# Attention values with the values as stationary operand, two branches in the two column halves, and sums transposed back

## The reference, cut to what matters

```python
s = jnp.einsum('bhgqd,bhqnkd->bhgqnk', qc, kg).astype(f32) * scale
p = masked_softmax(...)
o_sel = jnp.einsum('bhgqm,bhqmd->bhgqd', p, vg)
...
o_win = jnp.einsum('bhgcqk,bckhd->bcqhgd', p_w, vwin)
...
o_attn = gates[..., 0:1] * o_cmp + gates[..., 1:2] * o_sel + gates[..., 2:3] * o_win
```

## Time and profile before

| | |
|---|---|
| median of 3 runs | 605.27 us |
| lowest, highest | 604.96, 605.53 us |
| the profiled execution | 605.03 us |
| its span, first to last instruction | 603.3 us |
| granted TensorE clock over the span | 0.999 |
| PE busy | 591.7 us, 98% |
| DVE busy | 390.0 us, 65% |
| ACT busy | 299.9 us, 50% |
| POOL busy | 94.8 us, 16% |
| attention stage | 145.4 to 260.1 us |

### The profile page before, as it was taken

One profiled execution on the slowest core, in us unless ns is written; L12 is line 12 of the kernel. 1 busy time (PEld: TensorE's weight loads), 2 busy tenths in 40 slices (PEclk: granted clock), 3 DMA queues, 4 the chain that ended last, 5 costly groups with the idle time before them and its releaser, 6 DMA issues.

```text
span 603.3 us, 8925 instructions
## 1 busy us (share of the span) xinstructions
PE 591.7 (98%) x3009; PEld 494.1 (82%) x3009; DVE 390.0 (65%) x653; ACT 299.9 (50%) x533; POOL 94.8 (16%) x150
## 2 busy tenths in 40 slices
PE   8999999999999999999999999999999999999997
PEld 7777777888898889988888888888888888888885
DVE  3799862686688577656445434454368777788766
ACT  6865543638465667544323332233246555565561
POOL 1550000122222232222222122220000000000000
PEclk9999999999999999999999999999999999999999
DMA  8934247387878677777888888884326566555563
GB/s 308 325 94 140 93 160 252 108 290 186 240 147 226 141 148 211 116 181 170 246 222 205 262 199 230 216 201 122 105 92 200 197 185 197 174 153 179 193 207 139
DMA packets 33596, 112.51 MB, mean 186 GB/s; under 512 B 4560, under 2 KB 4848, under 8 KB 30752
## 3 DMA queue, kind: packets, MB, share of 16 engines
q1 hardware_dynamic: 28176, 72.56, 36.5%
q0 software_dynamic: 5248, 39.58, 28.7%
q10 hardware_dynamic: 144, 0.00, 0.0%
HBM read 110.03 MB, written 39.85 MB: 248 GB/s over the span
## 4 chain that ended last, share of the span: by engine, by line
PE 84%; DVE 6%; DMA 3%; issue 2%; POOL 2%; ACT 2%; SPq 1%; ACTq 0%; DVEq 0%
PE ps L356 23%; PE ps L358 23%; PE ps L357 23%; PE ps L1953 4%; PE ps L1941 2%; DMA xT<-in_xt 1%; PE ps L1903 1%; PE ps L1812 1%; PE ps L1904 1%; DMA pe_sb<-in_cmp_pe 1%; POOL rope_k L519 1%; PE ps L1669 1%; DVE ht_lo L1123 1%; PE ps L1775 1%; PE ps L1884 1%
## 5 line engine op out<-in xcount | busy, mean ns | idle before, releaser
L356 PE MATMUL ps<-ht_hi,w_hi_sb 128*128 128x512 f32 (+1 forms) x280 | 107.7, 385 | 0.0
L358 PE MATMUL ps<-ht_hi,w_lo_sb 128*128 128x512 f32 (+1 forms) x280 | 107.3, 383 | 0.0
L357 PE MATMUL ps<-ht_lo,w_hi_sb 128*128 128x512 f32 (+1 forms) x280 | 107.3, 383 | 0.0
L1030 ACT ACTIVATE w_hi_sb<-raw 128x1024 fp32r<-128x1024 f32 (+1 forms) x64 | 61.1, 954 | 61.1 <-PE ps L358 61.1
L1556 DVE TENSOR_TENSOR w_lo_sb<-raw,w_hi_sb 128x1024 fp32r<-128x1024 f32 (+1 forms) x64 | 68.5, 1089 | 32.5 <-ACT w_hi_sb L1030 32.3
L358 PE MATMUL ps<-w_hi_sb,a_lo 128*128 128x512 f32 x224 | 87.2, 389 | 0.0
L357 PE MATMUL ps<-w_lo_sb,a_hi 128*128 128x512 f32 x224 | 87.2, 389 | 0.0
L356 PE MATMUL ps<-w_hi_sb,a_hi 128*128 128x512 f32 x224 | 87.1, 389 | 0.0
L356 PE MATMUL ps<-w_hi_sb,ht_hi 128*128 128x512 f32 x192 | 81.6, 425 | 1.5 <-DVE w_lo_sb L1090 0.9
L1529 DVE TENSOR_TENSOR aq<-aq (+1 forms) x32 | 22.1, 692 | 86.3 <-ACT aq L1016 52.0
L358 PE MATMUL ps<-w_hi_sb,ht_lo 128*128 128x512 f32 x192 | 75.3, 392 | 0.0
(11 more groups left out here) (211 smaller groups left out, 922.3 us busy)
## 6 DMA issues: line engine op xcount, KB each, us to landing
raw<-in_w_ff SPq DMA_DIRECT2D x48, 512.0 KB, 4.3
forms<-in_w_ff POOLq DMA_DIRECT2D x32, 512.0 KB, 4.8
raw<-forms SPq DMA_DIRECT2D x32, 512.0 KB, 3.7
forms<-in_w_ff POOLq DMA_DIRECT2D x48, 256.0 KB, 4.8
raw<-in_w SPq DMA_DIRECT2D x23, 512.0 KB, 4.7
forms<-forms POOLq DMA_DIRECT2D x32, 256.0 KB, 5.0
xs<-in_x SPq DMA_DIRECT2D x8, 512.0 KB, 9.6
raw<-in_cmp_w SPq DMA_DIRECT2D x8, 512.0 KB, 4.5
```

What stands on the lines that cost most here:

```text
L356: pe.matmul(out, l_hi, r_hi, start=start, stop=False)
L357: pe.matmul(out, l_hi, r_lo, start=False, stop=False)
L358: return pe.matmul(out, l_lo, r_hi, start=False, stop=stop)
L1030: act.activation(w_hi_sb[:, FS[slot], 0:n], raw[:, slot, 0:n], ACT.Copy).then_inc(w_hi, 1)
```

## The change

The values of all steps but the last four are computed in another arrangement.

- Four steps (two heads, both branches) form a group `q` of 16; `QLAST` is 15, so 15 groups are new and the last four steps run in `last_values` as before, now into bank 6. The transposed probabilities of a group are kept in `pt_even` or `pt_odd`, eight slots in all.
- `values(q, ks)` (L1995 of the changed kernel): for each key tile `k` two products, one for each branch. The 64 columns of `v_sb` are the stationary operand, and the transposed probabilities of both heads move, 256 columns. The branch `b` writes to partitions `64 b` to `64 b + 63` of bank 7, in the column half `q % 2`. A group is cut into visits by `PARTS`: 1, 2, 3 and 3 of them for `t` = 0, 1, 2 and 3 (the last visit of `t = 3` takes two key tiles), one visit in a step.
- `ot(q)` on ACT (L980): copies the 128x256 sums to `ot_sb`, in the pass behind that of the last visit, after `exp(s + 2)` of that pass.
- `back(q)` on PE (L2014): two transposes of 128x128 from `ot_sb` to bank 6, so that the queries are in the partitions again. It waits for `ot_evac` and stands first in the second step behind the last visit, ahead of `scores(v + 2)`.
- `combine` reads bank 6 alone, waits for `back_done`, and moves to the passes 11, 19, 28, 36, 45, 53, 61 and 65 (before: 9, 17, 25, and so on). `norm_sum` and `norm_root` of the attention rows move with it: 19, 35, 51 to 20, 37, 54.

```diff
+GROUP = 4
+NQ = NV // GROUP
+QLAST = NQ - 1
+PARTS = {q: [[[0]], [[0], [1]], [[0], [1], [2]], [[0], [1], [2, 3]]][STEPS[GROUP * q][0]] for q in range(QLAST)}
+VALUES = {GROUP * q + GROUP - 1 + LAG + i: (q, ks) for q in PARTS for i, ks in enumerate(PARTS[q])}
+WHOLE = {q: GROUP * q + GROUP - 2 + LAG + len(PARTS[q]) for q in PARTS}
+BACK = {v + 2: q for q, v in WHOLE.items()}
+COMBINE = {v: q // 2 for v, q in BACK.items() if q % 2}
+COMBINE[NV + LAG - 1] = NQ // 2 - 1
...
             def pt(v):
                 n = P * (STEPS[v][0] + 1)
                 act.wait_ge(pt_done, v + 1)
-                if v >= 3:
-                    act.wait_ge(pv_done, v - 2)
-                act.activation(pt_sb[:, v % 3, 0:n], ps[:, 4 + v % 2, 0:n], ACT.Copy).then_inc(pt_evac[1], 1)
+                wait_pt_slot(act, v)
+                act.activation(pt_slot(v, n), ps[:, 4 + v % 2, 0:n], ACT.Copy).then_inc(pt_evac[1], 1)
+
+            def ot(q):
+
+                act.wait_ge(ot_done, q + 1)
+                if q >= 2:
+                    act.wait_ge(back_done, q - 1)
+                act.activation(ot_sb[:, q % 2, :, :].rearrange("p h s -> p (h s)"),
+                               ps[:, 7, q % 2 * 256:q % 2 * 256 + 256], ACT.Copy).then_inc(ot_evac, 1)
...
                 if w < NV:
                     exp(w)
+                if s - 1 in whole:
+                    ot(whole[s - 1])
                 if 0 <= s < NV and s % 2 == 1:
                     pt(s)
...
-                if s == 35:
+                if s == 37:
                     norm_root("attn", 0, 2)
-                if s == 51:
+                if s == 54:
                     norm_root("attn", 2)
...
-            def values(v):
+            def values(q, ks):
...
+                if ks[0] == 0:
+                    for b in range(NB):
+                        pe.wait_ge(pt_evac[b], 2 * q + 2)
...
+                for k in ks:
+                    for b in range(NB):
+                        pt = pt_odd[b] if q % 2 else pt_even[:, b, :, :]
+                        mm = pe.matmul(ps[HD * b:HD * b + HD, 7, cols], v_sb[:, k, b, g * HD:g * HD + HD],
+                                       pt[:, :, k * P:k * P + P], start=k == 0, stop=k == t)
+                if ks[-1] == t:
+                    mm.then_inc(ot_done, 1)
...
+            def back(q):
+
+                pe.wait_ge(ot_evac, q + 1)
...
+                if q % 2 == 0:
+                    wait_combined(q // 2)
+                for h in range(2):
+                    c = (q % 2 * 2 + h) * P
+                    mm = pe.transpose(ps[:, 6, c:c + P], ot_sb[:, q % 2, h, :], ident[:, :])
+                mm.then_inc(back_done, 1)
...
             for v in range(NV + LAG):
+                if v in BACK:
+                    back(BACK[v])
                 if v + LEAD < NV:
                     scores(v + LEAD)
...
-                if v >= LAG:
-                    values(v - LAG)
+                if v in VALUES:
+                    values(*VALUES[v])
+                if v - LAG >= GROUP * QLAST:
+                    last_values(v - LAG)
```

More of the change, by code:

```diff
@@ L132 @@
 SBANKS = 3
+GROUP = 4
[7 more added lines that the diff above has]
+COMBINE[NV + LAG - 1] = NQ // 2 - 1
+assert len(VALUES) == sum(map(len, PARTS.values())) and len(BACK) == QLAST and len(COMBINE) == NQ // 2
 PAIRED = NH * NB
@@ L263, in hybrid_block @@
         rope_sb = at("rope_sb", [P, NT, 2, HD], F32, o_gsgu + NG * HD * 4)
+        o_ones = area(0)
         ones = sb("ones", [P, P])
@@ L283, in hybrid_block @@
         pe_sb = sb("pe_sb", [P, 2, 16])
+        assert o_ones + 2 * SEQ * 4 <= top[0]
+        ot_sb = sb("ot_sb", [P, 2, 2, P])
         gate_t = at("gate_t", [GW, SEQ], F32, o_o + 3 * D * 4 + 2048)
@@ L402, in wait_out, with pt_slot, wait_pt_slot @@
                 eng.wait_ge(out_done, OUT_NO[s] + 1)
+        def pt_slot(v, n):
+            q, h, b = v // GROUP, v // 2 % 2, v % 2
+            return pt_odd[b][:, h, 0:n] if q % 2 else pt_even[:, b, h, 0:n]
+        def wait_pt_slot(eng, v):
+            if v >= 2 * GROUP:
+                eng.wait_ge(ot_done, v // GROUP - 1)
         def bc(ap, shape):
@@ L953, in job_act @@
                     ht_hi_evac(*k)
+            whole = {v: q for q, v in WHOLE.items()}
             exp(0)
@@ L1486, in _ @@
                     f_lo((s - 43) // 5, 2 * NS + (s - 43) // 5 + 1)
-                if s == 36:
+                if s == 38:
                     norm_inv("attn", 0, 2)
-                if s == 52:
+                if s == 55:
                     norm_inv("attn", 2)
@@ L1492, in _ @@
                     coefs(s // 16, s // 8 % 2)
-                if s >= 8 and s % 8 == 1:
-                    combine((s - LAG) // 16, (s - LAG) // 8 % 2)
+                if s in COMBINE:
+                    combine(COMBINE[s] // 2, COMBINE[s] % 2)
                 if s in (41, 45, 52, 56):
@@ L1942, in probs_t @@
                 mm.then_inc(pt_done, 1)
-            def values(v):
-                t, h, b = STEPS[v]
[L1946 to L1951, removed]
+            def values(q, ks):
+                t, h, _ = STEPS[GROUP * q]
+                g, cols = h // GQA, slice(q % 2 * 256, q % 2 * 256 + 256)
+                if ks[0] == 0:
+                    for b in range(NB):
+                        pe.wait_ge(pt_evac[b], 2 * q + 2)
+                    if q == 0:
+                        wait_free(pe, LAST_FILL[3])
+                    if q >= 2:
+                        pe.wait_ge(ot_evac, q - 1)
+                for k in ks:
[5 more added lines that the diff above has]
+                    mm.then_inc(ot_done, 1)
@@ new lines, in wait_combined @@
+            def wait_combined(group):
+                if group:
+                    pe.wait_ge(o_step, 5 * (group - 1) + 4)
+            def back(q):
+                pe.wait_ge(ot_evac, q + 1)
+                if q == 0:
+                    wait_free(pe, LAST_FILL[2])
+                if q % 2 == 0:
[4 more added lines that the diff above has]
+                mm.then_inc(back_done, 1)
@@ L1952, in values, with last_values @@
+            def last_values(v):
+                t, h, b = STEPS[v]
+                pe.wait_ge(pt_evac[b], v // 2 + 1)
+                wait_combined(NQ // 2 - 1)
+                c = h % 4 * P + b * HD
                 for k in range(t + 1):
-                    mm = pe.matmul(ps[:, 6 + h // 4, c:c + HD], pt_sb[:, v % 3, k * P:k * P + P],
-                                   v_sb[:, k, b, g * HD:g * HD + HD], start=k == 0, stop=k == t)
-                mm.then_inc(pv_done, 1)
+                    mm = pe.matmul(ps[:, 6, c:c + HD], pt_slot(v, SEQ)[:, k * P:k * P + P],
+                                   v_sb[:, k, b, h // GQA * HD:h // GQA * HD + HD], start=k == 0, stop=k == t)
+                mm.then_inc(pv_last, 1)
```

18 lines of the change are left out of this document (10 added, 8 removed).

## The result

The changed kernel takes **623.73 us** (median of 4 runs, 622.88 to 626.9) against 605.12 us (4 runs of the kernel before beside it, 604.93 to 605.53). The ratio is 1.0311, with a 95% interval of 1.0292 to 1.033: slower by 18.6 us, where the prediction said 11.3 us. The time lies in the predicted range, close to its upper end.

The account below looks back on a forecast made before the run. PE, busy for 98% of the span, was taken as the bound: 605.03 - 32.3 (old values) + 30.5 (new work) + 17.1 (waiting) - 4 (present stalls) gave 616.3 us, +11.3; range for 8 in 10: 606.5 to 624.

Parts of the forecast that it names:

- PE's own work: Attention stage: 32.3 us of old value records leave, 30.5 us of products, edges and transposes come; shrinks by 1.8 us.
- The edges: Entering and leaving the column halves on PE: 0.35 us for each of 33 visits, 11.6 us, priced from the L1812 block.
- The first rival: Faster, 602.7 us: edges cost nothing and the wait eats all 6 us of present stalls; chance 0.07.
- the second: Rival of no change, 604.4 us: edges at half price and only 11 us of the waiting left; chance 0.05.
- The wait: PE's `back` waits for ACT's copy behind scores, row maximum and exponential within one step, at 14 places: 17.1 us.
- the third rival: Worse, 626 us: the chain meets a busy DVE, 0.69 us at all 14 places, 9.7 us more; chance 0.12.
- DVE's 84% in tile 1: DVE busy for 23.07 of 27.5 us in attention tile 1, read as little room there.
- The relief: Small present PE waits in the attention stage fall away: 4 of an estimated 6 us go.
- The lower end: Least fall in present PE stalls: 1.5 us, what shows less the table load's wait.
- Edits at no cost: Probability slots, 15 ACT copies (5.7 us) and the moved `combine` add nothing beyond the chain; the stage's end is unchanged.

Follow-up runs that it names:

- both: The changed kernel with ACT's copy ahead of the exponential and PE's transposes back behind the projection piece, 33 visits: 606.19 us, ratio 1.0006 to the kernel before.
- fill_waits: The changed kernel with 86 more transposes of a constant tile on PE, ahead of the copy wait at groups 6 to 13: 621.28 us, ratio 1.0255.
- fewer_visits: `both` with 22 visits instead of 33 and the first MLP weight split moved to passes 44 and 46: 603.84 us, ratio 0.9967 to the kernel before.
- both_one_visit: `both` with all key tiles of a group in one visit, 15 visits instead of 33: 606.88 us, ratio 1.0019 to the kernel before.

## Why the prediction came out as it did

The sign, the mechanism and its place were right. The size was 6.6 us too small against the profiled execution (622.92 against 616.3). Term by term:

- **PE's own work, -1.8 us.** The work is right, and what failed is the assumption, never stated, that the clock stays. Busy time in the stage rose by 2.6 us. Of it 14 x 0.16 = 2.2 us belong to the waits (the part of a wait that hides under the record ahead of it, 0.27 us long where the next one starts 0.11 us after it), so the work came out at +0.4. That a 128-column weight load sets the pace of 0.11 us, for the value records as for the transposes, was my reading: the trace of before shows that distance with 64 columns moving (eight records in 1.00 us, each 0.27 long) and with 128 (four transposes in 0.60 us from 250.17), and no run changed the load alone. `both` shows PE's own work with neither the waits nor the half clock: -1.6 us. The 2 us between fit the two stretches at a granted clock of 0.50: `fill_waits`, which takes them away, is 2.45 us faster.
- **The edges, 0.35 us a visit.** The price came from one block; that it is due at each of the 33 visits was my assumption. Right at the single visit: 0.34 us. Taken over whole stages the price is a little lower, 0.28 us (`both` against `fewer_visits`); why is open. The first rival needed under 0.04, the second half the price. Both are out, and with them the 13.4 us that visits without edges would have saved.
- **The wait, 17.1 us.** Measured: 16.5 + 2.2 = 18.7 us, at the 14 places named. The 0.1 us for two hand-overs in each was an estimate that no row shows. At the longest wait the copy starts at 216.72, before the accumulator's read ends (216.63 + 0.19 = 216.82), and PE starts 0.06 us behind the copy's end (217.09). The parts differ more than the sum. Each with its 0.16 us, the first six waits have 4.1 us (forecast 5.2), the four before 384-column scores 7.6 (6.7), the last four 7.1 (5.2). The step that fell short here is the list of what stands ahead of the chain. I put the evacuation of a row tile there at step 40 only; it stands ahead of the waits behind steps 35 and 56 too (2.07 and 1.88 us), at the latter with a table load of ACT (1.28 us from 255.47). And the wait of 2.23 us, behind step 48, has ACT's part of a weight split in it, which I had left out:

```profile
235.53 0.14 DVE L1428 DVE_READ_ACCUMULATOR2_ANT nmax<- 128x1 f32 x1
236.11 1.05 ACT L954 ACTIVATE w_hi_sb<-raw 128x1024 fp32r<-128x1024 f32 x1
237.06 0.69 ACT L966 ACTIVATE p_sb<-ps,nmax 128x512 f32<-128x512 f32 x1
238.16 0.44 PE L2014 MATMUL ps<-ident,ot_sb 128*128 128x128 f32 x2 [2.23 <-ACT ot_sb L980]
```

The row maximum was done at 235.67, and the exponential starts at 237.06, behind the split. So here ACT was the busy engine, not DVE as in the third rival. DVE stands in the way at single places, with the low part of a row tile for one, and the 9.7 us for all 14 did not come. DVE's 84% in tile 1 was no sign: the waits there are among the shortest.
- **The relief, 4 us.** The step that failed most in its working. Waits for other things in the stage went from 3.0 to 1.2 us, 1.8 us of relief. The estimate of 6 us of present stalls had put 3 us on pieces too small to show, without a row. The lower end that I gave, 1.5, comes close by luck: it was to hold without the table load's wait of 1.21 us, which I had said would stay. That wait is the larger part of what went; why it went was not tested.
- **Edits at no cost.** The stage's end to the program's end is 343.2 us before and after, as predicted. The moved `combine` shows no wait of its own here, but it was no free move: with one visit a group, where it moves again, it met the split on DVE, and PE waited 2.4 us at that place; moving the split took 0.8 us of it back.

The differences are 1.6 (wait), 2.2 (relief), 2.2 (work, through the clock) and 0.6 us ahead of the stage, 6.6 us in all. The other three runs of the changed kernel had granted clocks of 0.996, 0.991 and 0.989 with 622.88, 624.55 and 626.9 us: the lower the clock the longer the run, so the half clock is likely to have a part in the wide spread. These three have no trace, so that is not shown.

## What to carry to other kernels

Where a new step needs a copy by another engine, look at what stands ahead of that copy in its queue: here the copy was 0.38 us long, PE lost 18.7 us to it in 14 waits, and exchanging two statements took back 14.7. List every side work of that engine in the passes concerned, too: a weight split and row tiles lengthened the chain at four of the 14 places at least. When a rearrangement shortens the array's own work by little, count the visits: the same 144 products in 22 visits instead of 33, with one weight split moved as well, were the difference between no gain and 0.3%. But fewer is not always better, since 15 visits shortened PE's work further and lost it again in waits. And when an operation moves because a table follows from another one (`combine` from `PARTS`), look up which work of its engine it lands beside.

## What the runs showed that was not expected

- TensorE's granted clock fell to 0.50 for 3.4 us at the end of waits of 2.07 and 2.70 us in the changed kernel and of one of 2.40 us in `both_one_visit`, but not at one of 2.23 us. Keeping PE busy with useless transposes in the waits held it at 1.00, and the kernel was 2.45 us faster. In the changed kernel the eleven waits of 0.3 to 1.9 us left the clock at 1.0. What sets the fall off is not shown.
- Two column halves overlap even when their records do not alternate, but late: the second half's first record started 0.92 us behind the first's, and the visit took 2.79 us, against 1.87 for the alternating order.
- Coming to the column halves and leaving them costs 0.34 us around four records, and 0.28 us a visit taken over whole stages (`both` against `fewer_visits`). What PE does in that time the traces do not show.
